# A decoder layer on one core: chunk sums of a gated linear attention in column strips, and split squares for its norm

## The reference, cut to what matters

```python
    b_last = b[:, :, -1]
    q_in = q * jnp.exp(b)
    k_in = k * jnp.exp(b_last[:, :, None] - b)
    chunk_kv = jnp.einsum('bnjhd,bnjhv->bnhdv', k_in, v)
    def step(S, xs):
        qc, dec, kv = xs
        o = jnp.einsum('bihd,bhdv->bihv', qc, S)
        S = jnp.exp(dec)[..., None] * S + kv
        return S, o
    ...
    o = rms_norm(o, gla_g).astype(h.dtype).reshape(B, T, D_GLA) * jax.nn.silu(r)
    out = jnp.concatenate([conv_out, o], axis=-1) @ w_out
```

## Time and profile before

| | |
|---|---|
| median of three runs | 1455.09 us |
| the profiled execution, its own time | 1453.73 us |
| its span (first to last instruction) | 1451.9 us |
| PE busy | 1429.9 us, 98% of the span |
| DVE, ACT, POOL busy | 589.3, 457.2, 385.5 us |
| in 338.0 to 370.3 us: PE, DVE, ACT, POOL busy | 32.30, 21.32, 22.34, 25.99 us |
| PE's longest idle times | 7.8 us at the start, 4.5 us at 217 us |

### The profile page before, as it was taken

One profiled execution on the slowest core, in us unless ns is written; L12 is line 12 of the kernel. 1 busy time (PEld: TensorE's weight loads), 2 busy tenths in 40 slices (PEclk: granted clock), 3 DMA queues, 4 the chain that ended last, 5 costly groups with the idle time before them and its releaser, 6 DMA issues.

```text
span 1451.9 us, 22458 instructions
## 1 busy us (share of the span) xinstructions
PE 1429.9 (98%) x9477; PEld 1399.9 (96%) x9477; DVE 589.3 (41%) x671; ACT 457.2 (31%) x618; POOL 385.5 (27%) x312
## 2 busy tenths in 40 slices
PE   7999998999999999999999999999999999999998
PEld 7899998998999999889999999999999999999997
DVE  5649999986533655623322111221112211122124
ACT  7662123447523433422232200221002310023224
POOL 6644321225322211003222222222222222222220
PEclk9999999999999999999999999999999999999999
DMA  8511350012523401771111111111111111111113
GB/s 340 166 50 58 53 51 30 30 30 77 204 102 123 153 31 38 264 252 44 59 44 43 44 58 43 44 43 45 57 43 43 43 46 55 44 43 43 44 43 117
DMA packets 47454, 114.11 MB, mean 79 GB/s; under 512 B 7769, under 2 KB 23449, under 8 KB 45985
## 3 DMA queue, kind: packets, MB, share of 16 engines
q1 hardware_dynamic: 47392, 113.22, 24.6%
HBM read 100.90 MB, written 12.30 MB: 78 GB/s over the span
## 4 chain that ended last, share of the span: by engine, by line
PE 86%; DVE 11%; ACT 1%; issue 0%; DMA 0%; POOL 0%; SPq 0%; DVEq 0%; ACTq 0%
PE ps L1259 59%; DVE ps L1949 8%; PE ps L1655 5%; PE ps L1362 5%; PE ps L1379 3%; PE m L1330 2%; PE ps L1689 2%; PE ps L1787 1%; PE ps L1608 1%; PE m L1568 1%; PE ps L1668 1%; PE m L1483 1%; PE m L1632 1%; PE ps L1599 1%; PE m L1581 1%; PE ps L1469 0%
## 5 line engine op out<-in xcount | busy, mean ns | idle before, releaser
L657 POOL TENSOR_TENSOR w_split<-w_raw,w_split 128x512 fp32r<-128x512 f32 x230 | 312.7, 1382 | 1003.0 <-ACT w_split L744 1002.9
L1259 PE MATMUL ps<-a_op,w_split 128*128 128x344 f32 x3168 | 499.4, 319 | 0.0
L1259 PEld LDWEIGHTS ps<-a_op,w_split 128*128 128x128 f32 x3168 | 497.8, 188 | 0.5 <-issue 0.5
L1259 PE MATMUL ps<-b_op,w_split 128*128 128x344 f32 x2304 | 362.6, 319 | 0.0
L1259 PEld LDWEIGHTS ps<-b_op,w_split 128*128 128x128 f32 x2304 | 361.7, 188 | 0.2
L1362 PE MATMUL ps<-a_op,w_split 128*128 128x344 f32 x1440 | 232.8, 321 | 0.0
L1362 PEld LDWEIGHTS ps<-a_op,w_split 128*128 128x128 f32 x1440 | 226.6, 188 | 0.4
L744 ACT ACTIVATE w_split<-w_raw 128x1024 fp32r<-128x1024 f32 x116 | 121.7, 1050 | 259.8 <-PE ps L1259 246.0
L1949 DVE SCALAR_TENSOR_TENSOR ps<-conv_in,par,ps 128x1024 f32<-128x1024 f32 x116 | 149.8, 1292 | 3.7
L2308 DVE SCALAR_TENSOR_TENSOR tmp<-ps,rstd 128x1032 f32<-128x1032 f32 x32 | 39.5, 1233 | 215.1 <-PE ps L1259 203.2
L2318 DVE TENSOR_TENSOR x_res<-x_res,ps 128x1032 f32 x24 | 29.5, 1230 | 230.8 <-PE ps L1259 230.8
(11 more groups left out here) (255 smaller groups left out, 1087.7 us busy)
## 6 DMA issues: line engine op xcount, KB each, us to landing
w_raw<-in_wt SPq DMA_DIRECT2D x117, 512.0 KB, 3.6
cache_b<-in_cache_v SPq DMA_DIRECT2D x8, 1024.0 KB, 11.9
x_in<-in_x SPq DMA_DIRECT2D x4, 1032.0 KB, 9.2
x_spill<-x_res SPq DMA_DIRECT2D x8, 516.0 KB, 2.6
w_more<-in_wt SPq DMA_DIRECT2D x8, 512.0 KB, 7.1
cache_a<-in_cache_k SPq DMA_DIRECT2D x2, 2048.0 KB, 11.7
cache_b<-in_cache_k SPq DMA_DIRECT2D x2, 2048.0 KB, 10.5
x_res<-in_x SPq DMA_DIRECT2D x1, 3096.0 KB, 10.2
```

Source lines behind the costliest of these rows:

```text
L657: gp.tensor_tensor(split(t, slot)[:, 1, part, :], src, split(t, slot)[:, 0, part, :].bitcast(F32), ALU.subtract).then_inc(w_low_done, 1)
L1259: last = pe.matmul(ps[:, c0 // CB, 0:w], w_split[:, slot, wp, k, :], src[:, k, xp, c0:c0 + w], start=(k == 0 and j == 0), stop=(k == KT - ...
```

## The change

Three things change together. First, `chunk_sum` makes four matmuls a chunk, one a head: 64 weight columns (a head's keys) by 128 columns of values, the two heads of a pair to PSUM partitions 0 to 63 and 64 to 127, in place of two matmuls of 128 by 256. Second, `state_after` handles a pair of heads in one instruction on 128 partitions. Third, the sums of squares are fp32r matmuls: ScalarE squares into `sq_raw`, copies to `sq_high` (fp32r), VectorE subtracts in place to `sq_low` (fp32r), and PE multiplies both parts with `ones_high`, 512 columns each, into one bank. `sums_of` now waits for `square_split`, which the subtraction signals, and it moved behind the next two chunk sums; `sums_of(3)` moved behind a piece of the first output tile.

```diff
-        sq_t = at("sq_t", (KT - 2) * 2 * T * 4, [P, H, T])
+        sq_low = at("sq_low", (KT - 2) * 2 * T * 4, [P, 2, H, 2 * C], F32R)
+        sq_high = at("sq_high", (KT - 2) * 2 * T * 4 + 2 * H * 2 * C * 4, [P, 2, H, 2 * C], F32R)
+        sq_raw = at("sq_raw", (KT - 2) * 2 * T * 4, [P, 2, H, 2 * C])
+        ones_high = at("ones_high", o2 - MEM * 4, [P, P], F32R)
...
@@ -1021,8 +1027,12 @@
             def square_round(r):
                 for par_ in range(2):
                     act.wait_ge(gla_products, 2 * r + par_ + 1)
-                    act.activation(round_cols(sq_t, r, par_), go_bank[r % 2][par_].rearrange("p (a n) -> p a n", a=2),
+                    act.activation(sq_raw[:, r % 2, par_:H:2, :], go_bank[r % 2][par_].rearrange("p (a n) -> p a n", a=2),
                                    ACT.Square).then_inc(gla_square, 1)
+                for par_ in range(2):
+                    act.wait_ge(gla_square, 2 * r + par_ + 1)
+                    act.activation(sq_high[:, r % 2, par_:H:2, :], sq_raw[:, r % 2, par_:H:2, :],
+                                   ACT.Copy).then_inc(square_high, 1)
...
+            act.activation(ones_high[:, :], ones[:, :], ACT.Copy).then_inc(ones_ready, 1)
...
-                    pe.wait_ge(state_ready, 4 * (c - 1))
-                for pair in range(2):
-                    last = pe.matmul(PS[0][:, c % 2, pair * 256:(pair + 1) * 256], k_in[:, c, pair, :],
-                                     v_tok[:, c, pair * 256:(pair + 1) * 256], start=True, stop=True)
+                    pe.wait_ge(state_ready, 2 * (c - 1))
+                for h in range(H):
+                    rows, pair = slice(DK * (h % 2), DK * (h % 2 + 1)), h // 2
+                    last = pe.matmul(PS[0][rows, c % 2, pair * DV:(pair + 1) * DV], k_in[:, c, pair, rows],
+                                     v_tok[:, c, h * DV:(h + 1) * DV], start=True, stop=True)
                 last.then_inc(chunk_kv, 1)
...
-                    pe.wait_ge(gla_square, 2 * (r + 1))
-                    fill(("sum", r, pair), lambda bank: pe.matmul(bank[:, :].rearrange("p (b n) -> p b n", b=2), ones[:, :],
-                                                                  sq_t[:, 2 * pair:2 * pair + 2, NS + 2 * C * r:NS + 2 * C * (r + 1)],
-                                                                  start=True, stop=True))
+                    def ops(bank):
+                        for part in (sq_high, sq_low):
+                            last = pe.matmul(bank[:, :].rearrange("p (b n) -> p b n", b=2), ones_high[:, :],
+                                             part[:, r % 2, 2 * pair:2 * pair + 2, :], start=part is sq_high, stop=part is sq_low)
+                        return last
+                    pe.wait_ge(ones_ready, 1)
+                    pe.wait_ge(square_split, r + 1)
+                    fill(("sum", r, pair), ops)
...
             chunk_sum(3)
             outputs(1)
-            sums_of(0)
             chunk_sum(4)
             chunk_sum(5)
+            sums_of(0)
             outputs(2)
-            sums_of(1)
             chunk_sum(6)
             chunk_sum(7)
+            sums_of(1)
             pe.wait_ge(gla_state_loaded, 16)
...
             tile_product(t, t % 2, a_op, ALL[:2], wait_conv, range(0, 2))
+            pe.wait_ge(gla_square, 2 * NR)
+            tile_product(t, t % 2, a_op, ALL[2:], no_wait, range(0, 2))
             sums_of(3)
-            tile_product(t, t % 2, a_op, ALL[2:], no_wait, range(0, 2))
             pe.wait_ge(sample_squared, 1)
             fill(("smp_sum", 0), lambda bank: pe.matmul(bank[:, 0:H * NS], ones[:, :], sample_norm, start=True, stop=True))
             tile_product(t, t % 2, a_op, ALL, wait_conv, range(2, CT))
...
-                for h in range(H):
-                    p0, pair = DK * (h % 2), h // 2
-                    kvp = PS[0][p0:p0 + DK, c % 2, h * DV:(h + 1) * DV]
+                for pair in range(2):
+                    kvp = PS[0][:, c % 2, pair * DV:(pair + 1) * DV]
...
+                        dve.tensor_copy(state[:, 0, pair, :], kvp).then_inc(state_ready, 1)
...
-                        dve.scalar_tensor_tensor(out=state[p0:p0 + DK, c, pair, :], in0=state[p0:p0 + DK, c - 1, pair, :],
-                                                 scalar=small[p0:p0 + DK, pair * NC_ + c:pair * NC_ + c + 1], in1=kvp,
+                        if pair == 0:
+                            dve.wait_ge(state_ready, 2 * c)
+                        dve.scalar_tensor_tensor(out=state[:, c, pair, :], in0=state[:, c - 1, pair, :],
+                                                 scalar=small[:, pair * NC_ + c:pair * NC_ + c + 1], in1=kvp,
                                                  op0=ALU.mult, op1=ALU.add).then_inc(state_ready, 1)
...
+            def square_low(r):
+                dve.wait_ge(square_high, 2 * (r + 1))
+                dve.tensor_tensor(sq_low[:, r % 2, :, :], sq_raw[:, r % 2, :, :],
+                                  sq_high[:, r % 2, :, :].bitcast(F32), ALU.subtract).then_inc(square_split, 1)
...
             gate_round(1)
             state_after(4)
+            square_low(0)
             state_after(5)
             gate_round(2)
             state_after(6)
+            square_low(1)
             state_after(7)
             bank, b, _ = misc(("smp", 0))
             wait_full(dve, ("smp", 0))
             dve.tensor_copy(o_strip[:, :], bank[:, 0:DV]).then_inc(misc_free[b], 1)
+            square_low(2)
             gate_round(3)
             bank, b, _ = misc(("smp_turn", 0))
...
+            square_low(3)
             dve.engine_nop().then_inc(sample_out_read, 1)
```

More of the change, by code:

```diff
@@ L308, in build @@
         gla_square = sem("gla_square")
+        square_high = sem("square_high")
+        square_split = sem("square_split")
+        ones_ready = sem("ones_ready")
         gla_rstd = sem("gla_rstd")
@@ L1470, in outputs @@
                                      sc_t[:, pair, c, par_, :], start=(j == 0), stop=False)
-                pe.wait_ge(state_ready, 4 * (2 * r + 1))
+                pe.wait_ge(state_ready, 2 * (2 * r + 1))
                 for j, c, pair, par_ in parts:
@@ L1934, in _ @@
             n_taps = 0
-            conv_acc =            n_taps = 0
             conv_acc = PS[1][:, 0:2, :]
@@ L2053, in state_after @@
                 dve.wait_ge(chunk_kv, c + 1)
-                for h in range(H):
-                    p0, pair = DK * (h % 2), h // 2
-                    kvp = PS[0][p0:p0 + DK, c % 2, h * DV:(h + 1) * DV]
+                for pair in range(2):
+                    kvp = PS[0][:, c % 2, pair * DV:(pair + 1) * DV]
                     if c == 0:
-                        if h == 0:
+                        if pair == 0:
                             dve.wait_ge(decays_ready, 1)
                             dve.wait_ge(q_updated, 16)
-                        dve.tensor_copy(state[p0:p0 + DK, 0, pair, :], kvp).then_inc(state_ready, 1)
+                        dve.tensor_copy(state[:, 0, pair, :], kvp).then_inc(state_ready, 1)
                     else:
-                        if h == 0:
-                            dve.wait_ge(state_ready, H * c)
-                        dve.scalar_tensor_tensor(out=state[p0:p0 + DK, c, pair, :], in0=state[p0:p0 + DK, c - 1, pair, :],
-                                                 scalar=small[p0:p0 + DK, pair * NC_ + c:pair * NC_ + c + 1], in1=kvp,
+                        if pair == 0:
+                            dve.wait_ge(state_ready, 2 * c)
+                        dve.scalar_tensor_tensor(out=state[:, c, pair, :], in0=state[:, c - 1, pair, :],
+                                                 scalar=small[:, pair * NC_ + c:pair * NC_ + c + 1], in1=kvp,
                                                  op0=ALU.mult, op1=ALU.add).then_inc(state_ready, 1)
```

2 lines of the change are left out of this document (1 added, 1 removed).

## The result

The changed kernel takes 1465.88 us (median of 4 runs, 1465.37 to 1466.0), the kernel before 1455.04 us (4 runs on the same chip, 1454.71 to 1455.58). The ratio is 1.0072, 95% interval 1.0059 to 1.0085: 10.8 us slower. The forecast was 1462.5 us with a range of 1458.0 to 1466.5, and 0.88 for slower. So the sign held and the time lies in the range, close to its upper end; the forecast's shift of 7.4 us is 3.4 us short of the measured one.

A forecast was written before the change was run, and what follows sets the result against it. PE was taken as the bound. Waits of 4.35 + 3.3 + 0.6 + 3.4 less 5.4 us of work gave 6.25; plus 1.6 less 0.45 slack made 7.4 us, so 1455.09 + 7.4 = 1462.5 us, range 1458.0 to 1466.5.

The forecast's parts named there:

- What bounds the kernel: Whole kernel and GLA stage: PE is busy 98% of the span, so PE work removed or PE waits count their length.
- the 7 us below which the prediction called itself wrong: GLA stage: the prediction is wrong if PE's idle time there is below 7 us.
- PE's work that goes: PE up to the end of `outputs(3)`: 0.5 + 3 x 0.74 + 3 x 0.90 = 5.4 us less work.
- The waits: PE stands 4.35, 3.3 and 3.4 us before sums of rounds 0 to 2, 0.6 us before the samples' product.
- three `sq_low` longer than 1.22 us: VectorE's subtractions in the profile after: three lengthened by the wait for GpSimd, the fourth not.
- The wait for GpSimd: VectorE's subtraction, both inputs in SBUF, waits to the end of GpSimd's running instruction; GpSimd's undisturbed low parts take 2.36 us each.
- GpSimd coming second in round 0: Rival: VectorE's subtraction goes before GpSimd's start, PE stands 2.45 us there; shift 5.55 us, 1460.6 us; chance 0.17.
- Behind `outputs(3)`: After `outputs(3)`, copies and subtraction make the chain to `gla_low` 1.6 us longer, less 0.45 us of slack.
- the clock falls in the waits: Rival: PE's clock halves after long waits; one fall gives 1463.9 us, three give 1466.7; chance 0.13.
- No exclusion at all: Rival: VectorE's subtractions never wait for GpSimd; stalls total 7.3 us, shift 3.05 us, 1458.1 us; chance 0.12.
- Strips do not overlap: Rival: chunk sums in strips of 64 columns save nothing on PE; 2.7 us more, 1465.2 us; chance 0.05.
- Faster: Rival: squares are split in time and PE stands nowhere; -4.2 us, 1450.9 us; chance 0.05.

The follow-up runs named there:

- the kernel with filled waits: The changed kernel with 16, 11 and 12 needless fp32r matmuls in PE's waits of rounds 0, 1 and 2: 1462.41 us.
- the first experiment: The kernel before with only the chunk sums in column strips and the states by pairs, squares, sums and order as before: 1453.22 us.
- both engines reordered: The changed kernel with sums a round later, samples' product behind `outputs(3)` and sums of round 0, and VectorE's `gate_round(3)` ahead of its read of that product: 1453.84 us.
- the kernel without GpSimd's reads: The changed kernel with eight GpSimd instructions (four convolution low parts, four samples' states) turned into memsets that only write: 1460.85 us.
- the kernel with earlier subtractions: The changed kernel with only VectorE's subtractions of rounds 1 and 2 moved earlier in its queue: 1462.41 us.
- the later order without reads: The changed kernel with each round's sums a round later on PE, and GpSimd's eight instructions turned into memsets that only write: 1454.59 us.

## Why the prediction was right, and what it missed

**What bounds the kernel: right.** The stage grew by 10.5 us and the kernel by 10.8. Nothing behind the stage took up the loss. PE's idle time in the stage, 9.85 us up to the sums of round 2, is above the 7 us below which the prediction called itself wrong.

**PE's work that goes: 5.4 us forecast, 4.95 measured.** The nearest row for a pair in strips was good (1.09 us taken, 1.02 measured, 345.66 - 344.64 in the kernel after too), and a round's four sums take 0.92 to 1.01 us at full clock for the 0.92 taken. In the kernel with filled waits `outputs(3)` ends at 372.36, which is 372.36 - 339.64 = 32.72 us after the first chunk sum, for 365.23 - 338.46 = 26.77 before: 5.95 us later. Its waits come to 10.9, so 4.95 us of work went. The 0.45 us that lack are of the size that the strips alone lacked in their stage (2.2 for 2.7), where the rows show them at the array's change between full width and strips.

**The waits: right within 0.3 us each, and all too long.** In the kernel with filled waits, from the end of the chunk sums (or the samples' product) to the first sum: 353.65 - 349.43 = 4.22 us for 4.35 forecast, 361.68 - 358.65 = 3.03 for 3.3, 0.41 for 0.6, 368.39 - 365.14 = 3.25 for 3.4. Their sum is 10.9 for 11.65. So two errors, 0.75 us too much waiting and 0.45 too much work saved, partly cancel, and the forecast comes nearer to this kernel (7.4 us of shift for 7.16 in the stage and 7.8 in the medians) than its terms do. Its subtractions take 3.18, 1.99, 2.81 and 1.23 us: three long ones and a short one, as forecast.

In the kernel after itself they are 4.08, 2.19, 0.40 and 3.18, and the second subtraction takes 1.22. The condition "three `sq_low` longer than 1.22 us" is thus met by two. With `outputs(2)` at half speed VectorE's gate of that round came later, and GpSimd had finished its four at 360.71 before VectorE asked at 362.67.

**The wait for GpSimd: right.** The prediction took all of it, against a rival with none. Without GpSimd's reads every subtraction is 1.22 or 1.23 us, beside GpSimd's writes too; with them it is up to 3.41, in the kernel with the split alone. The rule of the Trainium skill (SBUF — State Buffer, Who interferes with whom), that two such instructions exclude each other, agrees with these runs. What the trace also shows is that the instruction in progress is waited for nearly to its end: VectorE's row goes from 350.69 to 353.81, and the first of GpSimd's four, 2.36 us long when undisturbed, runs from 350.32 to some 352.68. GpSimd coming second in round 0 did not happen: it started at 350.32, 0.37 us ahead of VectorE.

**Behind `outputs(3)`: right.** The end of the stage shifts by 7.16 us in the kernel with filled waits (55.01 - 47.85), 1.2 more than the end of `outputs(3)`; forecast were 1.6 less 0.45, 1.15. In the kernel after it is the same: 376.04 - 339.97 = 36.07 us for 26.77, 9.3 later, and 10.5 at the end. The last `gla_low`, which was to come 7 to 8 us later, comes 7.2 later in the kernel with filled waits and 10.5 in the kernel after.

**The step that was wrong: the clock.** The prediction named it as a rival, "the clock falls in the waits", and gave it 0.13, with 1.4 us for one fall and 4.2 for three; the sum itself holds nothing for it. What it held against it was that the waits are shorter than the one of 4.55 us. That was the wrong reason: the clock fell behind waits of 4.08 and 3.18 us here, and in other runs behind 2.54, 2.19 and 1.59. It fell twice, not in all three long waits, and the first fall was dearer than the one it was priced from, since PE was busy at half speed for 6.1 us and not 2.8. Those two falls cost 4.5 us. They also gave back 1.05 in shorter waits (9.85 us for the four that take 10.9 at full clock), so the net is some 3.4 us, for 3.1 to 3.5 measured with the waits filled. By the forecast's own arithmetic the kernel without them was to take 1462.5 us. The measured time lies in the range because the range's upper end had been drawn nearly up to three falls; the step from 1462.5 to 1465.9 is this rival come true, in part and at a price of its own, and not the forecast.

**The other rivals.** No exclusion at all was to give 1458.1 us; with the reads gone it was 1460.85, of which 1.7 us were a fall of the clock. "Strips do not overlap" fell with the first experiment. "Faster" needed PE to stand nowhere; even with both engines reordered the gain was 1.3 us (1455.13 - 1453.84) and not 4.2.

**What stays open.** When the clock falls was not settled. In the kernel after, a wait of 2.19 us in round 1 left it at 1.00, while one of 2.19 us in round 0 of the kernel without GpSimd's reads was followed by a fall 1.5 us after PE had gone on; and after 4.08 and 4.07 us of waiting in two kernels it was low for 6.8 us in one and for some 3.4 in the other (the kernel with earlier subtractions, whose windows from 350 to 360 us show 0.87 and 0.78; 1.3 and 2.2 us at half). The wait of 4.5 us at 217 us, which no kernel here changes, likewise had 3.4 us at half behind it in five profiles and 6.7 in six. So part of what the clock costs one execution is chance, and one profile does not give its size. The runs of one kernel differ in it as well: 1452.9 to 1456.9 us in the later order without reads. The rest of the strips' price at each change of width was seen in neighbouring rows and was not taken apart.

## What to carry to other kernels

A new link between two engines costs what the receiving engine cannot do meanwhile. Splitting an operand saved PE 0.9 us a round and put two copies and a subtraction between its source and its use, in a queue that cannot pass a wait. With a round's worth of other work ahead of the consumer the same instructions went from 10.8 us lost to 1.3 us gained, which is what the strips give alone: the waits were hidden, but the split itself earned nothing. Where TensorE is made to stand, price the clock too, by the work that follows the wait: here waits of 4.08 and 3.18 us were followed by slow stretches that lost another 4.5 us. And look at what an instruction with two SBUF inputs meets on GpSimd: 1.22 us became 1.9 to 3.4.

## What the runs showed of the hardware

- After a wait the granted clock was 0.50 for 6.8 us in one place of the stage and for 3.4 us in others. Behind one and the same wait of 4.5 us at 217 us it was 0.50 for 3.4 us in five profiles and for 6.7 us in six (0.88 and 0.76 over 14 us).
- The clock also fell behind waits of 2.19 and 1.59 us, more than 1 us after PE had gone on, and stayed at 1.00 behind another wait of 2.19 us.
- Needless matmuls in TensorE's waits held its clock at 1.00 and made the kernel 3.1 to 3.5 us faster with 39 matmuls more.
- A VectorE subtraction with both inputs in SBUF took 1.22 us beside a GpSimd instruction that only writes, and 1.9 to 3.4 us beside GpSimd instructions that read.
- A pair of chunk sums in strips of 64 columns takes 1.02 us for 1.83, but the fp32 group behind it takes 0.10 us longer (1.98 for 1.88) and the group ahead 0.09 (1.91 for 1.82).
- A VectorE update of 128 x 128 elements with one PSUM input costs 1.43 / 4 = 0.36 us, no more than one of 64 x 128 (0.38).
